# Mixer one: level of ones merged into the keys of the level of twos, gates a chunk ahead, one meeting between stages, earlier down weights in the last unit

## The reference, cut to what matters

```python
def hgrn2_mixer(h, lb, w_in, norm_g, w_out):
    q, f, i, g = jnp.split(h @ w_in, 4, axis=-1)
    log_f = jnp.logaddexp(jnp.log(lb), jnp.log1p(-lb) + jax.nn.log_sigmoid(heads(f)))
    k = (1.0 - lb) * jax.nn.sigmoid(-heads(f))
    qh = jax.nn.silu(heads(q)) * (HGRN_DK ** -0.5)
    o = gated_chunkwise(qh, k, heads(i), log_f)
    o = rms_norm(o, norm_g) * jax.nn.silu(heads(g))
    return o.reshape(b, t, d) @ w_out

# in a chunk, G = cumsum(log_f):  scores[i,j] = sum_d q[i,d] k[j,d] exp(G[i,d] - G[j,d]),  j <= i
# o = scores @ v + (q exp(G)) @ state;  state = exp(G_last) state + (k exp(G_last - G))^T v
```

## Time and profile before

| | |
|---|---|
| median of 3 runs | 5099.4 us (5096.78 to 5100.18) |
| the profiled execution's own time | 5100.33 us |
| its span | 5098.5 us |
| TensorE (PE) | busy 4976.2 us, 98%; mean granted clock 0.988 |
| VectorE (DVE) | busy 2818.6 us, 55% |
| ScalarE (ACT) | busy 840.1 us, 16% |
| 2107 to 2860 us (mixer one and 34 us of the FFN) | PE busy 726.78 us of 753.00 |
| 2860 to 5098.5 us (experts) | PE busy 2188.44 us of 2238.50 |

### The profile page before, as it was taken

One profiled execution on the slowest core, in us unless ns is written; L12 is line 12 of the kernel. 1 busy time (PEld: TensorE's weight loads), 2 busy tenths in 40 slices (PEclk: granted clock), 3 DMA queues, 4 the chain that ended last, 5 costly groups with the idle time before them and its releaser, 6 DMA issues. The chain is left out here.

```text
span 5098.5 us, 66831 instructions
## 1 busy us (share of the span) xinstructions
PE 4976.2 (98%) x25703; PEld 3332.0 (65%) x25703; DVE 2818.6 (55%) x4948; ACT 840.1 (16%) x1623; POOL 70.4 (1%) x96
## 2 busy tenths in 40 slices
PE   8999999999999999999999799999999999999998
PEld 4545556755444444447666595969778696969694
DVE  3434445544333333553666475757667575757686
ACT  3611211133100000160445100000000000000010
POOL 0000000000000000000000000000000000000110
PEclk9999999999999999999999799999999999999999
DMA  5145033411211122443222254554545455545575
GB/s 206 42 153 172 25 108 101 158 44 59 62 41 49 41 95 97 147 118 124 101 75 74 100 197 139 179 177 142 182 150 188 153 183 173 182 173 195 194 260 214
DMA packets 363793, 672.34 MB, mean 132 GB/s; under 512 B 18200, under 2 KB 142171, under 8 KB 361434
## 3 DMA queue, kind: packets, MB, share of 16 engines
q1 hardware_dynamic: 349272, 619.78, 35.0%
q0 software_dynamic: 9920, 36.19, 1.9%
q10 hardware_dynamic: 4290, 12.11, 0.6%
HBM read 564.20 MB, written 103.82 MB: 131 GB/s over the span
## 5 line engine op out<-in xcount | busy, mean ns | idle before, releaser
L4603 PE MATMUL psum<-arena 128*128 128x128 f32 (+2 forms) x10752 | 1236.2, 277 | 6.3 <-issue 4.9
L4603 PEld LDWEIGHTS psum<-arena 128*128 128x128 f32 x10752 | 1225.6, 191 | 11.1 <-issue 11.1
L4582 PE MATMUL psum<-arena 128*128 128x512 f32 x1568 | 691.5, 597 | 8.7 <-DVE arena L4195 8.7
L4312 DVE TENSOR_TENSOR arena<-arena 128x1024 f32<-128x1024 f32 x448 | 539.5, 1224 | 64.7 <-issue 39.4
L4582 PEld LDWEIGHTS psum<-arena 128*128 128x128 f32 x1568 | 292.9, 190 | 370.4 <-issue 364.1
L1449 PE MATMUL psum<-arena 128*128 128x512 f32 x1120 | 480.8, 592 | 0.0
L1449 PEld LDWEIGHTS psum<-arena 128*128 128x128 f32 x1120 | 212.8, 190 | 267.9 <-issue 267.9
L1499 PE MATMUL psum<-arena 128*128 128x512 f32 x616 | 265.0, 592 | 0.0
L1998 PE MATMUL psum<-arena 128*128 128x256 f32 (+1 forms) x968 | 241.2, 409 | 1.9 <-PEq L101 1.9
L4487 ACT ACTIVATE arena<-psum 128x288 f32<-128x288 f32 (+1 forms) x112 | 44.6, 398 | 1167.7 <-PE psum L4603 1128.4
L4603 PE MATMUL psum<-gate_row,arena 128*128 128x128 f32 (+2 forms) x1792 | 221.3, 277 | 4.3 <-DVE arena L4379 4.3
(11 more groups left out here) (619 smaller groups left out, 5797.1 us busy)
## 6 DMA issues: line engine op xcount, KB each, us to landing
arena<-in_moe_w_gate SPq DMA_DIRECT2D x112, 1024.0 KB, 7.2
arena<-in_moe_w_up SPq DMA_DIRECT2D x112, 1024.0 KB, 7.3
arena<-in_moe_w_down SPq DMA_DIRECT2D x112, 1024.0 KB, 5.3
y_dram<-zeros SPq DMA_DIRECT2D x1, 23040.0 KB
x_dram<-arena SPq DMA_DIRECT2D x32, 512.0 KB, 4.0
arena<-in_ab_w_in SPq DMA_DIRECT2D x7, 2048.0 KB, 9.1
arena<-z_dram SPq DMA_DIRECT2D x8, 1664.0 KB, 7.6
arena<-in_c_w_in SPq DMA_DIRECT2D x6, 2048.0 KB, 12.8
```

Source lines behind the costliest of these rows:

```text
L4312: V.tensor_tensor(to, left, right, ALU.subtract).then_inc(t_up, 1)
L4582: return nc.tensor.matmul(g.ps[:, bank, :], left, right, start=(i == 0), stop=(i == STEPS - 1))
L4603: last = nc.tensor.matmul(g.ps[:, bank, f * HT:f * HT + N // 2], right[:, k, f * P:(f + 1) * P], left[:, k, 0:N // 2], start=(k == 0), sto ...
```

## The change

1. **Scores.** The level of ones is no longer a level: L is 6. Of the diagonal only the even queries are computed by `scores(c, 0)`, eight heads, 64 columns read with a stride of two from `q`. `scores(c, 6)` and `(c, 7)`, four heads each, multiply keys that serve three purposes by 128 columns. The keys `kl[1]` hold, in even tokens, the decayed keys written against the odd token next to them, in odd tokens a plain copy of `kc`; the columns `pair_q` are the 64 queries of the level of twos and the 64 odd queries (`take_odd`). There are 56 matmuls in a chunk where there were 64. The level of ones' `differences`, `exps` and `queries` go; ScalarE gains two copies of 128x512 a chunk. `pick` 0 becomes one copy with stride two; picks 6 and 7 are two copies of 128x256 each with a drain between them.
2. **Gates a chunk ahead.** Chunk 0 runs gates(0) in the four early places and gates(1) in the late places, where the other chunks have `outputs`; chunk c runs gates(c + 1) early; chunk 7 runs none. `hc` is one buffer, so SP loads the next one after the gates that read it.
3. **One meeting.** `chained_stage` clears the semaphores of the stage before at the start of the next, so that only the meeting at the block's end is left. It is used by the first five stages; before the experts `end_chain` clears and meets as before.
4. **Last unit's homes.** `x_part` moves to `wraw[3]`, the ring to `grow`, a late part of `hid`, a half of `wraw[2]` and `axial`. The first two down loads are issued at h = 8 and 9; `grow` (the final norm's gain) is loaded after the tiles.

```diff
@@ stage
+def chained_stage(nc, name, past, *sems):
+    handles = [nc.alloc_semaphore(f"{name}_{s}") for s in sems]
+    if past:
+        nc.clear_and_free_semaphores(past)
+    past[:] = handles
+    with nc.Block() as block:
+        yield (block, *handles)
+
+def end_chain(nc, past):
+    nc.clear_and_free_semaphores(past)
+    past.clear()
+    nc.all_engine_barrier()
@@ mixer_one_stage
-    F, H, L, HALF = KD, KD, NLEV - 1, P // 2
+    F, H, L, HALF = KD, KD, NLEV - 2, P // 2
-    hc = [A.at(45056 + 1024 * b, KD, P) for b in range(2)]
+    hc = A.at(45056, KD, P)
+    pair_q = A.at(46080, F, P)
+    ql = [A.at(17408, F, HALF), pair_q[:, :, 0:HALF]]
@@ sync
+                if c == 0:
+                    sp.wait_ge(gg_done, 2)
+                    sp.dma_start(hc, g.ht_dram[1]).then_inc(h_in[1], 16)
                 if c + 2 < NT:
-                    sp.wait_ge(gg_done, 2 * c + 2)
-                    sp.dma_start(hc[c % 2], g.ht_dram[c + 2]).then_inc(h_in[c % 2], 16)
+                    sp.wait_ge(gg_done, 2 * c + 4)
+                    sp.dma_start(hc, g.ht_dram[c + 2]).then_inc(h_in[c % 2], 16)
@@ tensor
-                if i < 2:
-                    for h in range(4):
-                        last = nc.tensor.matmul(g.ps[:, n % 2, h * P:(h + 1) * P], kc[c % 2][:, 4 * i + h, :], q[c % 2][:, 4 * i + h, :], start=True, stop=True)
+                if i == 0:
+                    even = halves(q[c % 2], 1)[0]
+                    for h in range(H):
+                        last = nc.tensor.matmul(g.ps[:, n % 2, h * HALF:(h + 1) * HALF], kc[c % 2][:, h, :], even[:, h, :, 0], start=True, stop=True)
+                elif i >= L:
+                    pe.wait_ge(ql_made, level(c, L) + 1)
+                    pe.wait_ge(odd_made, c + 1)
+                    for h in range(4):
+                        own = 4 * (i - L) + h
+                        last = nc.tensor.matmul(g.ps[:, n % 2, h * P:(h + 1) * P], kl[1][:, own, :], pair_q[:, own, :], start=True, stop=True)
...
+            def early_slot(c, i):
+                if c == 0:
+                    gates(0, i)
+                elif c + 1 < NT:
+                    gates(c + 1, i)
+
+            def late_slot(c, i):
+                if c == 0:
+                    gates(1, i)
+                elif c <= NT:
+                    outputs(c - 1, i)
@@ scalar
+                if m == L:
+                    nc.scalar.activation(halves(kl[1], 1)[1], halves(kc[c % 2], 1)[1], ACT.Copy)
...
+            def take_odd(c):
+                act.wait_ge(q_in[c % 2], 16 * (c // 2 + 1))
+                if c:
+                    act.wait_ge(sc, S * c)
+                nc.scalar.activation(pair_q[:, :, HALF:P], halves(q[c % 2], 1)[1][:, :, :, 0], ACT.Copy).then_inc(odd_made, 1)
@@ expert_stage
-    ring, junk = [wraw[1][:, 0, :], wraw[1][:, 1, :], wraw[3][:, 0, :], g.axial.rearrange("p a t r -> p (a t r)")], A.at(45184, 512)
+    ring, junk = [grow, late_hid, wraw[2][:, 1, :], g.axial.rearrange("p a t r -> p (a t r)")], A.at(45184, 512)
-    xr, x_part, square_of = xg[:, 0:2, :], wraw[0], wraw[2][:, 0, :]
+    xr, x_part, square_of = xg[:, 0:2, :], wraw[3], wraw[2][:, 0, :]
-                    if not last and 8 <= h < 8 + RAW - 1:
+                    if 8 <= h < 8 + (FREE if last else RAW - 1):
                         load_down(h - 8)
...
-                    for i in range(RAW - 1):
+                    for i in range(FREE, RAW - 1):
                         load_down(i)
+                    sp.dma_start(grow, rows(I["final_norm_g_2"])).then_inc(g.x_back, 16)
```

More of the change, by code:

```diff
@@ L2906, in level, with scored_by @@
         return L * c + m - 1
[L2908 to L2910 removed]
+    def scored_by(lev):
+        return S * (lev // L) + lev % L + (2 if lev % L < L - 1 else 3)
     def x_bank(t):
@@ L3003, in _ @@
             sp.dma_start(x[0], g.x_dram[0:P, :]).then_inc(x_in[0], 16)
-            for c in range(2):
-                sp.dma_start(hc[c], g.ht_dram[c]).then_inc(h_in[c], 16)
+            sp.dma_start(hc, g.ht_dram[0]).then_inc(h_in[0], 16)
             for n in range(2):
@@ L3086, in gates @@
                     pe.wait_ge(wg_in[n], 16)
-                    if c >= 2:
-                        pe.wait_ge(xadded, 2 * (c - 2) + n + 1)
+                    if c >= 3:
+                        pe.wait_ge(xadded, 2 * (c - 3) + n + 1)
+                    elif c:
+                        pe.wait_ge(gate_made, 2 * (c - 1) + n + 1)
                 for k in range(k0, k0 + 4):
-                    last = nc.tensor.matmul(g.ps[:, 6 + n, :], hc[c % 2][:, k, :], wg[n][:, k, :], start=(k == 0), stop=(k == KD - 1))
+                    last = nc.tensor.matmul(g.ps[:, 6 + n, :], hc[:, k, :], wg[n][:, k, :], start=(k == 0), stop=(k == KD - 1))
                 if k0:
@@ L3233, in _ @@
                     scores(c, 0)
+                    early_slot(c, 0)
+                    turn_keys(c)
                     scores(c, 1)
-                    gates(c, 0)
-                    turn_keys(c)
+                    early_slot(c, 1)
                     scores(c, 2)
-                    gates(c, 1)
-                    scores(c, 3)
                     keys_values(c)
@@ L3245, in _ @@
                 if now:
-                    gates(c, 2)
-                    scores(c, 4)
+                    early_slot(c, 2)
+                    scores(c, 3)
                 if last_but and now:
@@ L3250, in _ @@
                 if now:
-                    gates(c, 3)
+                    early_slot(c, 3)
+                    scores(c, 4)
+                late_slot(c, 0)
+                if now:
                     scores(c, 5)
[L3253 to L3257, removed]
-                    outputs(c - 1, 1)
+                late_slot(c, 1)
                 if last_but and c <= NT:
@@ L3261, in _ @@
                 if now:
-                    scores(c, 7)
+                    scores(c, 6)
                 if last_but and c <= NT:
                     logits(c - 2)
-                if before:
-                    outputs(c - 1, 2)
+                late_slot(c, 2)
                 if now:
-                    scores(c, 8)
+                    scores(c, 7)
                 if c == NT:
                     turn_x(NT - 1, 0, KD // 2)
-                if before:
-                    outputs(c - 1, 3)
+                late_slot(c, 3)
                 if c == NT + 1:
@@ L3574, in _ @@
                     pick(c, 0)
-                    pick(c, 1)
                 if c == NT:
@@ L3582, in _ @@
                     differences(c, 3)
-                    pick(c, 2)
+                    pick(c, 1)
                 if last_but and c != NT:
@@ L3588, in _ @@
                     differences(c, 4)
-                    pick(c, 3)
+                    pick(c, 2)
                     update(c)
@@ L3592, in _ @@
                     differences(c, 5)
-                    pick(c, 4)
+                    pick(c, 3)
                 if c + 1 < NT:
@@ L3598, in _ @@
                     differences(c, 6)
-                    pick(c, 5)
+                    pick(c, 4)
                 if c + 1 < NT:
@@ L3603, in _ @@
                     queries(c, 6)
-                    differences(c, 7)
-                    pick(c, 6)
+                    pick(c, 5)
                 if before:
@@ L3610, in _ @@
                 if now:
-                    queries(c, 7)
-                    pick(c, 7)
+                    pick(c, 6)
                 if last_but:
@@ L3618, in _ @@
                 if now:
-                    pick(c, 8)
+                    pick(c, 7)
         @block.scalar
@@ L3794, in _ @@
                     key_exps(c + 1)
-                if now:
-                    exps(c, 7)
                 if c + 1 < NT:
                     exps(c + 1, 1)
+                if c == 0:
+                    take_gates(1)
 def layer_one_mixer(nc, g, I):
```

81 lines of the change are left out of this document (53 added, 28 removed).

## The result

The changed kernel takes 5071.62 us (median of 6 runs, 5070.03 to 5076.1) against 5099.31 us (6 runs, 5096.78 to 5100.18) of the kernel before: ratio 0.9949, 95% interval 0.9939 to 0.9959, 27.7 us less. The forecast was 5073.6. The profiled execution took 5070.03 us, with a span of 5068.2.

The account below looks back on a forecast made before the run. TensorE, busy 98% of the span, was taken to bound the kernel inside the chunks. Mixer one 15.9 + meetings 3.0 + last unit 7.4 - contention 0.5 = 25.8 us gained, giving 5073.6 us; range 5067 to 5087, 8 in 10.

Parts of the forecast that it names:

- Part 1: Scores in mixer one: with 128 keys the stationary side sets the price; a full chunk gains 1.74 us.
- The rival by columns: Scores: moving columns set the price, 0.88 us less in eight chunks, total 5080.6 us; chance 0.05.
- the rival of a longer chain: VectorE's longer chain, pick drains or the stride eat 15 us or more: 5090, or 5115 us; chance 0.04.
- Part 2: Gates a chunk ahead: chunk 0 takes 46.2 us, 2.3 more; chunk 7 takes 41.9, 7.6 less, despite idling 4.9.
- The wait for `hc`: Chunk 0: chunk 1's hc loads only after gates(0, 3), so TensorE loses 2.2 us.
- The wait of `turn_x`: Chunk 7: turn_x waits for line 3771's copy behind turn_out, 0.9 us with the semaphores.
- Part 3: Stage boundaries: four lose the distance between two meetings, 2.4 to 3.6 us, taken as 3.0.
- Part 4: Last unit: early down loads start the down part sooner and at full clock; gain 7.4 us, less 0.5 contention.
- The two waits behind the start: Last unit's down part: TensorE waits 1.1 us for the_others, and the next sums hold step 1 by 0.1 to 0.2.
- The contention of 0.5 us: Last unit: early down loads share DMA engines with tiles and up weights; between zero and 7.4 us, taken as 0.5.
- The rival that the last unit gives nothing: The early down loads bring no gain in the last unit, total 5080.5 us; chance 0.10.
- The two rivals of a lasting half clock: Half clock after chunk 7's gap lasts to 30 us (5083.6 us, chance 0.10) or through the tail (5117, 0.03).

Follow-up runs that it names:

- number 12: The changed kernel, unaltered, run again on one chip: 5073.02 us, ratio 0.9947.
- number 4: The kernel before with only the gates a chunk ahead and the single hc, scores as before: 5098.92 us, ratio 1.0003.
- number 3: The kernel before with only the new scores and picks, gates in their own chunk: 5085.97 us, ratio 0.9976.
- number 11: The changed kernel with each chunk's gates made in that chunk again: 5075.31 us, ratio 0.9954.
- Number 5: The changed kernel with chunk 1's hc loaded ahead of the loop into a home of its own: 5068.06 us, ratio 0.9942.
- number 1: The kernel before with only the chained stages, one meeting at four boundaries: 5098.87 us against 5098.68, ratio 0.9999.
- number 10: The changed kernel with the old stage boundary of two meetings: 5080.74 us, ratio 0.9966.
- 6: The changed kernel with the second half of chunk 7's gates left in chunk 7: 5071.55 us, ratio 0.9948.
- 7: The changed kernel with chunk 1's hc in its own home and the second half of chunk 7's gates left in chunk 7: 5068.27 us, ratio 0.9941.
- Number 2: The kernel before with only the last unit's two early down loads and the homes they need: 5090.87 us, ratio 0.9985.
- number 8: The changed kernel with one early down load in place of two (FREE = 1): 5072.01 us, ratio 0.9949.
- number 9: The changed kernel with chunk 1's hc home, half of chunk 7's gates left there, chunk 6's Silu copy before the exponentials: 5065.25 us, ratio 0.9934.

## Why the prediction was right

The direction and the time held, and with them the price of the scores, the gap in chunk 7 and the earlier down steps. The clock behind short waits was left out, and the gain of one meeting is not settled. That the sum comes within 2 us is luck in part: between the two profiles the loop gave 15.2 us for a forecast 15.9, the experts 10.5 for 6.9, and the rest 4.6 for 3.0. Step by step:

**Part 1, forecast 1.74 us a full chunk.** Measured 1.78. The reading of the earlier trace rows held: the stationary side sets the price, and a stride of two in float32 costs nothing beside it. The rival by columns is out: it gave 0.88. The Trainium skill (TensorE: Matmul & The Clock Gate, Back-to-back issue gap) gives formulas by the moving columns, but says first that in a stream of weight loads and matmuls both set the spacing, which the prediction passed over. The trace agrees with that and not with the columns alone: twice the columns, 1.88 us for 1.84 in the same place. No wait for a pick shows in the full chunks, so the rival of a longer chain is out as well.

**Part 2, chunk 0 forecast 46.2, chunk 7 41.9.** Measured 47.38 and 41.58, and 45.89 and about 41.8 in number 12. The wait for `hc` was put at 2.2 and is 1.66 to 1.87. What I left out is the clock behind it, though the earlier trace rows had it at 0.50 behind waits of 1.6 us. In the changed kernel it fell after 1.66 us of idle time and cost 1.7 us; in number 12, the same kernel, it did not after 1.87 us:

```profile
2459.90 3.70 PE L3122 MATMUL psum<-arena 128*128 128x512 f32 x8 [1.87 <-DMA arena<-ht_dram]
```

Six profiles have this wait. Behind 1.66, 1.68, 1.71 and 1.90 us the gates took 5.1 to 5.2 us, behind 1.73 and 1.87 the usual 3.5. So the length of the wait does not tell the price, and 2.28 us do not either (number 4). In chunk 7 the gap was put at 4.9 and is 4.92, half clock at 2.3 and is 1.9. The wait of `turn_x` for the copy of line 3771, 0.9, did not come; the queries of the next level kept TensorE 0.65 us instead.

**What was booked in the wrong place.** The sum gave the chunks at both ends, 5.3 us net, to the gates. They give nothing there as they stand: the loop is 405.1 us with the scores alone (number 3) and with both, and the kernel before with the gates alone is not faster (number 4). Against number 3 the gates cost 6.2 us in chunk 0 (41.16 to 47.38) and give 6.2 in chunk 7 and the tail (79.6 to 73.4). The end chunks' gain belongs to the scores: 2.7 us in chunk 0 and 1.4 in chunk 7 with the tail. My accounting compared chunk 0 with before, where it had idle time, and counted the scores' gain into the gates' price. By medians the gates may still be worth 2.3 us (number 11), inside the uncertainty. Number 5 points at what they could be worth once a side effect is removed: it takes 3.6 us off chunk 0, 2.1 against number 12.

**Part 3, forecast 3.0 us.** Not settled in size. In the kernel before, one meeting shows nothing (number 1, 4.6 either way). In the changed kernel it is worth 7.7 us (number 10). The forecast counted the distance of two meetings and left the clock out.

In mixer zero the clock counts. The stage, from the last meeting ahead of it to the first behind it, takes 620.7 to 621.8 us in the four profiles where two meetings brought the clock down, 619.85 in number 3, where it held behind two, and 619.2 to 619.9 in the nine with one meeting.

In mixer one it does not. With one meeting TensorE waits 1.73 us ahead of its first product, with two 2.33. But 17 us behind the meeting it stands still for ScalarE in either case, and goes on only 0.4 us sooner (17.03 for 17.40), whether it had started at half clock or not. In three profiles, the changed kernel's of the result among them, the clock fell behind that second wait, 1.9 us long; in numbers 6, 7 and 12 it did not behind the same wait. In the three chunk 0 begins 294.7 us behind the meeting; in the other six with one meeting 293.0, with two meetings 293.4.

So the traces of numbers 10 and 12 account for some 5 of the 7.7 us: 2.9 of distances, 1.9 in mixer zero, 0.4 in mixer one. The rest stays open. Stages whose code is the same scatter by 2 to 4 us between profiles (the front stage 343.3 and 344.5, attention 389.2 and 392.2 in the changed kernel's two). By the medians the four parts alone give 7.8, 12.7, -0.2 and -0.2 us, 20.1 together, and the whole 27.7, in number 12 24.8. The 5 to 8 us between are about what one meeting gives in number 10 and not in number 1; no run shows why.

**Part 4, forecast 6.9 us.** Number 2 has 7.6 (3 to 12), the expert stage of the profiles 10.5. Over all profiles the stage takes 2241.7 to 2244.5 us without this part (four) and 2230.3 to 2235.5 with it (ten), 9.5 between the means, so the term was too small. The terms of the 10.5: the gap 7.2 less (forecast 6.5 sooner and two short waits), and the up part 0.65 and the down part 0.95 us shorter; the other 1.8 lie ahead of the last unit. The start at full clock held here (1.00 for 0.78), but not by the reason given, a wait of only 2.2 us. The gap was shorter, 1.55. Of the ten profiles, seven have gaps of 1.46 to 1.66 us and full clock behind them; in numbers 2, 7 and 12 the gap was 2.11, 2.38 and 2.38 us, and the clock stood at 0.50 for 3.4 us. Number 12, timeline of PE and a window:

```profile
4974.95 85.99 PE L4648 MATMUL psum<-arena 128*128 128x512 f32 x196 [2.38 <-DVE arena L4261]
```

```profile
4975.00:4978.00 3.00, 3.00 (x4) 1.45 (x5) 2.49 (x7) 0.00 (x0) 0.00 (x0) 0.50 1.01 401
```

The two waits behind the start were put at 1.1 and 0.1 to 0.2 and are 0.44 and 0.30 in the profile of the result. The contention of 0.5 us is not to be seen. The rival that the last unit gives nothing is out.

**The two rivals of a lasting half clock** needed a clock that stays at 1.2 GHz well behind chunk 7's gap. It was back 4.0 us after TensorE's restart. In the six profiles with this gap it took 4.0 to 7.2 us, and the longest (number 8) made chunk 7 1.5 us longer, not 8. The Trainium skill (TensorE: Matmul & The Clock Gate, HAM oscillation) describes waits for loads that bring the clock down each time. The trace agrees for the wait of 4.9 us, in six profiles of six. Shorter ones go either way: it fell behind 1.66 us in one profile, and not behind 1.87 in another.

## What to carry to other kernels

When a moved block fills idle time at one end of a loop and opens some at the other, compare the loop with and without the move, holding the rest of the change fixed; a comparison of chunks with the old kernel credits it with gains that are another part's. A gap on TensorE has two prices, its length and the clock behind it, and the second is not certain: state both. In a full schedule taking work out moves the wait to the next engine's list: before moving a ScalarE copy, look which table it needs and what stands around it.

## What the runs showed of the hardware

**The clock behind a stage boundary.** The fourteen profiles taken, by how the engines meet (granted clock in the first 2.5 us behind the last meeting):

```
                      two meetings (5 profiles)   one meeting (9 profiles)
start of attention    below 0.65 in 3             1.00 in all
start of mixer zero   below 0.85 in 4             1.00 in all
start of the FFN      1.00 in all                 1.00 in all
start of mixer one    0.50 to 0.54 in all         0.65 to 0.67 in 3, 1.00 in 6
```

TensorE idled 0.6 us less at mixer one's start with one meeting, 1.73 for 2.33. The fall can also only come later: at attention's start 5 us behind the meeting in five of the nine, at 0.50 to 0.56, and in mixer one 18 us behind it in three of the six. That the shorter idle time keeps the clock up fits the counts; it was not tried by itself.

**Table loads.** In number 9 ScalarE's table load takes 1.28 us, begins 0.02 us after the activation before it ends, and is followed by the next 0.01 to 0.02 us later. The Trainium skill (ScalarE: Activation LUTs, What ACT_TABLE_LOAD costs) has the same 1.28 us and a drain of 1.38 beside it. The drain is not in these rows.
